# Values and keys of an attention stage as three products of upper and lower parts, in a hybrid decoder step

## The reference

```
z   = x @ w_in                                # 384 query latents | 256 kv latents | 32 rope
ckv = rms_norm(z[..., 384:640], kv_norm)
q   = (rms_norm(z[..., :384], q_norm) @ w_q_up)   # 16 heads x (64 + 32)
s   = q_nope . (ckv @ w_uk[h]) + rope(q) . rope(k), causal, softmax -> p
out = (p @ (ckv @ w_uv[h])) @ w_o
```

## Time and profile before

| what | value |
|---|---|
| median of 3 executions | 1387.92 us (lowest 1387.88) |
| the profiled execution: time | 1389.12 us |
| the profiled execution: span in the trace | 1387.0 us |
| PE busy | 1366.7 us, 99% of the span |
| DVE, ACT, POOL busy | 643.7, 518.8, 258.5 us (46%, 37%, 19%) |
| mean granted TensorE clock | 0.997 |

### The profile page before, as it was taken

The page is one execution under the profiler, slowest core; times in us unless marked ns, Lnnn a source line. Parts: engine busy times, 40 slices in busy tenths (PEclk is TensorE's granted clock), DMA queues, the critical chain, the costliest instruction groups (busy, mean ns, idle before and its releaser), DMA issues.

```text
span 1387.0 us, 26630 instructions
## 1 busy us (share of the span) xinstructions
PE 1366.7 (99%) x10422; PEld 1281.9 (92%) x10422; DVE 643.7 (46%) x934; ACT 518.8 (37%) x838; POOL 258.5 (19%) x350
## 2 busy tenths in 40 slices
PE   9999999999999999999999999999999999999997
PEld 9867777669999999999999999999999999999996
DVE  4556666433752232133233778877432322333335
ACT  4256666332442221122223388854422212222224
POOL 0052222001550000000003415665400000000033
PEclk9999999999999999999999999999999999999998
DMA  8231110242233332222332213132223322332301
GB/s 223 65 97 30 30 22 14 67 148 61 66 87 91 102 99 86 62 79 73 102 126 69 69 36 101 62 115 71 79 75 102 126 61 61 91 90 88 110 1 65
DMA packets 180867, 111.13 MB, mean 80 GB/s; under 512 B 25928, under 2 KB 179101, under 8 KB 180800
## 3 DMA queue, kind: packets, MB, share of 16 engines
q1 hardware_dynamic: 180208, 109.41, 27.1%
q0 software_dynamic: 592, 0.79, 0.2%
HBM read 107.15 MB, written 3.02 MB: 79 GB/s over the span
## 4 chain that ended last, share of the span: by engine, by line
PE 90%; DVE 5%; ACT 2%; issue 1%; SPq 0%; POOL 0%; DMA 0%; DVEq 0%; ACTq 0%; POOLq 0%
PE ps L556 55%; PE ps L585 8%; PE ps L648 4%; PE ps L837 3%; PE ps L850 2%; PE ps L810 1%; PE ps L873 1%; PE ps L1163 1%; PE ps L827 1%; PE ps L1052 1%; PE ps L1215 1%; PE ps L919 1%; PE ps L1074 1%; PE ps L1015 1%; PE ps L1186 1%
## 5 line engine op out<-in xcount | busy, mean ns | idle before, releaser
L556 PE MATMUL ps<-xh,wl 128*128 128x280 f32 x1472 | 310.5, 292 | 0.0
L556 PE MATMUL ps<-xh,wh 128*128 128x280 f32 x1472 | 308.8, 291 | 0.7 <-ACT sg L1579 0.7
L556 PE MATMUL ps<-xl,wh 128*128 128x280 f32 x1472 | 307.8, 290 | 0.0
L1284 ACT ACTIVATE wh<-raw 128x2048 fp32r<-128x2048 f32 (+2 forms) x78 | 161.1, 2065 | 198.6 <-PE ps L556 179.5
L556 PEld LDWEIGHTS ps<-xh,wh 128*128 128x128 f32 x1472 | 233.9, 188 | 1.3 <-ACT sg L1579 1.1
L556 PEld LDWEIGHTS ps<-xh,wl 128*128 128x128 f32 x1472 | 234.6, 189 | 0.0
L1669 DVE TENSOR_TENSOR wl<-raw,wh 128x2048 fp32r<-128x2048 f32 (+2 forms) x78 | 195.9, 2511 | 79.1 <-ACT wh L1284 79.0
L556 PEld LDWEIGHTS ps<-xl,wh 128*128 128x128 f32 x1472 | 232.1, 188 | 0.0
L2033 DVE TENSOR_TENSOR ht<-sg,ps 128x560 f32<-128x560 f32 x44 | 32.5, 738 | 268.9 <-PE ps L556 264.8
L2228 POOL TENSOR_TENSOR acc<-xT 128x560 f32<-128x560 f32 x4 | 7.7, 1933 | 745.7 <-DVE xT L1919 648.5
L1581 ACT ACTIVATE hh<-ht 128x560 f32 (+1 forms) x44 | 29.6, 672 | 262.1 <-DVE ht L2033 262.1
(11 more groups left out here) (361 smaller groups left out, 2576.4 us busy)
## 6 DMA issues: line engine op xcount, KB each, us to landing
raw<-in_ffn_w_gu SPq DMA_DIRECT2D x176, 256.0 KB, 3.7
raw<-in_ffn_w_down SPq DMA_DIRECT2D x48, 384.0 KB, 4.2
raw<-in_lru_w_in SPq DMA_DIRECT2D x16, 512.0 KB, 4.6
Ctok<-in_cache_latent SPq DMA_DIRECT2D x48, 128.0 KB, 2.2
raw<-in_mla_w_o SPq DMA_DIRECT2D x16, 256.0 KB, 3.7
raw<-in_ffn_w_down SPq DMA_DIRECT2D x16, 256.0 KB, 5.1
raw<-in_lru_w_o SPq DMA_DIRECT2D x16, 256.0 KB, 3.4
wq<-in_mla_w_q_up SPq DMA_DIRECT2D x16, 144.0 KB, 2.3
```

Of the source, the lines that this page charges most:

```text
L556: mm = pe.matmul(ps[:, 1024 * jp + 512 * h:1024 * jp + 512 * h + TH], w[:, k, col:col + P], x[:, k, h * TH:(h + 1) * TH], start=(k == 0 an ...
L1284: act.activation(wh[u][:, 0:w], raw[u][:, 0:w], ACT.Copy).then_inc(hi_ok, 1)
```

## The change

The values of token tiles 1 to 4 and all keys are computed from parts, as three products with float32r operands, in place of one float32 product. For this:

- ACT makes `wuvh` and DVE `wuvl`, each 128 x 2048, in the two `raw` buffers (these are free from the split of chunk 1 and of chunk 2 on). The load of `wuv` signals `in_cst` now; waits on `in_att` and `in_cst` are renumbered.
- ACT makes `kvh` and DVE `kvl` of the two normed kv latent tiles, in the places of tiles 6 and 7 of `xh` and `xl`. DVE first waits for the end of chunk 2 (`t1_ok` 3).
- POOL makes `wukh` and `wukl` for each pair, in `key_weights(p)`. `keys(p)` waits for `s_kp2` in place of the load. POOL's start is put in another order: the two first `swap`s and `key_weights(0)` come ahead of the copies into `K` and of the rows out.
- SP waits for all ten groups of values (`s_v` 10) ahead of samples 2 and 3, since their pages overwrite `wuvh` and `wuvl`.

The semaphore counts that moved with it (`s_z`, `s_zroot`, `s_kp2`, `d_new`) follow from these. Diff, with unchanged lines cut:

```
@@ -197,6 +197,12 @@
+        wuvh = place("wuvh", [P, KC, HEADS * VH], F32R, raw_at + 4 * W_MAX)[0]
+        wuvl = place("wuvl", [P, KC, HEADS * VH], F32R, raw_at)[0]
+        wuk_parts = raw_at + 4 * (W_MAX + PAGES * KV_R)
+        wukh, wukl = (place(f"wuk{s}", [P, KC, P], F32R, wuk_parts + 4 * KC * P * i)[0] for i, s in enumerate("hl"))
+        kvh, kvl = (t[:, KD - KC:KD, :] for t in (xh, xl))
+
         Ctok = [put(f"Ctok{s}", [P, PAGES, KV_R]) for s in range(2)]
@@ -419,7 +425,7 @@
             sp.dma_start(trig[:], c_trig).then_inc(in_att, 16)
-            sp.dma_start(wuv[:], mla_w_uv[0].rearrange("(k p) h v -> p k (h v)", p=P)).then_inc(in_att, 16)
+            sp.dma_start(wuv[:], mla_w_uv[0].rearrange("(k p) h v -> p k (h v)", p=P)).then_inc(in_cst, 16)
             sp.dma_start(pages[:], page_table.rearrange("b n -> (b n)").rearrange("(a n) -> a n", a=1)).then_inc(in_pg, 16)
@@ -466,6 +472,7 @@
             sp.wait_ge(lo_ok, 3)
+            sp.wait_ge(s_v, 10)
             for b in range(2, 4):
@@ -780,7 +787,7 @@
-            pe.wait_ge(in_att, 32)
+            pe.wait_ge(in_cst, 48)
             pe.wait_ge(s_z, KC)
@@ -807,8 +814,17 @@
                     for k in range(KC):
-                        mm = pe.matmul(ps[0:n, bank:bank + 512], z[:, KQ + k, kt * P:kt * P + n],
-                                       wuv[:, k, h * 512:(h + 1) * 512], start=(k == 0), stop=(k == KC - 1))
+                        if kt == 0:
+                            mm = pe.matmul(ps[0:n, bank:bank + 512], z[:, KQ + k, kt * P:kt * P + n],
+                                           wuv[:, k, h * 512:(h + 1) * 512], start=(k == 0), stop=(k == KC - 1))
+                            continue
+                        if g == 2:
+                            pe.wait_ge(s_ste, 2)
+                            pe.wait_ge(s_z, KC + k + 1)
+                        for i, (x, w) in enumerate(((kvh, wuvh), (kvl, wuvh), (kvh, wuvl))):
+                            mm = pe.matmul(ps[0:n, bank:bank + 512], x[:, k, kt * P:kt * P + n],
+                                           w[:, k, h * 512:(h + 1) * 512], start=(k == 0 and i == 0),
+                                           stop=(k == KC - 1 and i == 2))
                     mm.then_inc(s_v, 1)
@@ -819,13 +835,15 @@
-                pe.wait_ge(wuk_in, (p + 1) * 16)
+                pe.wait_ge(s_kp2, p * 2 + 4)
                 if above_zero(p):
...
                     for k in range(KC):
-                        mm = pe.matmul(ps[:, 512 * (6 + h):512 * (6 + h) + NP // 2], wuk[:, k, :],
-                                       z[:, KQ + k, h * (NP // 2):(h + 1) * (NP // 2)], start=(k == 0), stop=(k == KC - 1))
+                        for i, (w, x) in enumerate(((wukh, kvh), (wukh, kvl), (wukl, kvh))):
+                            mm = pe.matmul(ps[:, 512 * (6 + h):512 * (6 + h) + NP // 2], w[:, k, :],
+                                           x[:, k, h * (NP // 2):(h + 1) * (NP // 2)], start=(k == 0 and i == 0),
+                                           stop=(k == KC - 1 and i == 2))
                 mm.then_inc(k_sum, 1)
@@ -975,14 +993,14 @@
             pe.wait_ge(s_lte, 2)
-            pe.wait_ge(s_z, 2 * KQ + KC)
+            pe.wait_ge(s_z, 2 * KQ + 2 * KC)
             for n in range(2):
...
             pe.wait_ge(s_vd, 5)
-            pe.wait_ge(s_kp2, 2)
+            pe.wait_ge(s_kp2, 4)
             pe.wait_ge(s_cb, 3)
@@ -994,7 +1012,7 @@
             pe.wait_ge(q_rot, HEADS)
-            pe.wait_ge(in_att, 64)
+            pe.wait_ge(in_att, 48)
             pe.wait_ge(d_new, 3)
@@ -1320,6 +1338,10 @@
                 act.activation(zsq[:, tile, :], z[:, tile, :], ACT.Square).then_inc(s_zsq, 1)
+                if c == 1:
+                    act.wait_ge(in_cst, 48)
+                    act.wait_ge(lo_ok, 2)
+                    act.activation(wuvh[:], wuv[:], ACT.Copy).then_inc(s_parA, 1)
                 act.wait_ge(f1_ok, c + 1)
@@ -1332,6 +1354,9 @@
             act.activation(zsq[:, 2, :], z[:, 2, :], ACT.Square).then_inc(s_zsq, 1)
+            for k in range(KC):
+                act.wait_ge(s_z, k + 1)
+                act.activation(kvh[:, k, :], z[:, KQ + k, :], ACT.Copy).then_inc(s_zroot, 1)
             def row_tile(t):
@@ -1355,7 +1380,7 @@
                     for k in range(KQ):
-                        act.wait_ge(s_z, KC + k + 1)
+                        act.wait_ge(s_z, 2 * KC + k + 1)
                         act.activation(zqh[k][:], z[:, k, :], ACT.Copy).then_inc(s_zroot, 1)
@@ -1738,12 +1763,14 @@
+            dve.wait_ge(s_parA, 2)
+            dve.tensor_tensor(wuvl[:], wuv[:], wuvh[:].bitcast(F32), ALU.subtract).then_inc(s_ste, 1)
             latents(1)
...
                 dve.tensor_scalar(halves(stat[:, n, :]), pair(jp), EPS, None, ALU.add).then_inc(s_zeps, 1)
-                dve.wait_ge(s_zroot, n + 1)
+                dve.wait_ge(s_zroot, 1 + n * (1 + KC))
                 dve.reciprocal(stat[:, n, :], stat[:, n, :]).then_inc(s_zinv, 1)
@@ -1752,7 +1779,7 @@
             normed(0, 2, range(KQ, KQ + KC))
-            dve.wait_ge(in_att, 32)
+            dve.wait_ge(in_att, 48)
             dve.wait_ge(t0_ok, 3)
@@ -1760,6 +1787,10 @@
                 dve.tensor_tensor(krs[r:r + 32, :], rt[:, 0, :], rt[:, 1, :], ALU.add).then_inc(s_kr, 1)
+            dve.wait_ge(t1_ok, 3)
+            for k in range(KC):
+                dve.wait_ge(s_zroot, 2 + k)
+                dve.tensor_tensor(kvl[:, k, :], z[:, KQ + k, :], kvh[:, k, :].bitcast(F32), ALU.subtract).then_inc(s_z, 1)
             for g in range(1, 10, 2):
@@ -1770,7 +1801,7 @@
                     for k in range(KQ):
-                        dve.wait_ge(s_zroot, 3 + k)
+                        dve.wait_ge(s_zroot, 3 + KC + k)
                         dve.tensor_tensor(zql[:, k, :], z[:, k, :], zqh[k][:].bitcast(F32), ALU.subtract).then_inc(s_z, 1)
@@ -2136,7 +2167,7 @@
-            pool.wait_ge(in_cst, 32)
+            pool.wait_ge(in_cst, 48)
             pool.wait_ge(in_id, 16)
@@ -2144,11 +2175,9 @@
             pool.wait_ge(s_cb, 3)
-            pool.wait_ge(s_z, KQ + KC)
+            pool.wait_ge(s_z, KC)
             pool.tensor_copy(zn[:], z[:, KQ:KQ + KC, NP:T]).then_inc(d_new, 1)
-            pool.wait_ge(d_new, 1)
-            for s in range(2):
-                pool.tensor_copy(K[s][64:P, :], krs[64:P, 0:NP]).then_inc(s_kp2, 1)
+            pool.memset(Qs[:], 0.0).then_inc(d_new, 1)
@@ -2163,9 +2192,6 @@
-            for t in range(2):
-                rows_out(t)
-
             def swap(h, u):
@@ -2185,11 +2211,26 @@
-            pool.wait_ge(s_kp2, 2)
-            pool.memset(Qs[:], 0.0).then_inc(d_new, 1)
+            def key_weights(p):
+
+                pool.wait_ge(wuk_in, (p + 1) * 16)
+                if p > 0:
+                    pool.wait_ge(k_sum, p)
+                pool.tensor_copy(wukh[:], wuk[:]).then_inc(s_kp2, 1)
+                pool.wait_ge(s_kp2, 1 if p == 0 else p * 2 + 3)
+                pool.tensor_tensor(wukl[:], wuk[:], wukh[:].bitcast(F32), ALU.subtract).then_inc(s_kp2, 1)
+
             for u in range(2):
...
                 swap(u, u)
+            key_weights(0)
+            pool.wait_ge(s_z, KQ + 2 * KC)
+            pool.wait_ge(s_kp2, 2)
+            for s in range(2):
+                pool.tensor_copy(K[s][64:P, :], krs[64:P, 0:NP]).then_inc(s_kp2, 1)
+            for t in range(2):
+                rows_out(t)
+            pool.wait_ge(s_kp2, 4)
             pool.wait_ge(s_ve, 5)
@@ -2199,6 +2240,7 @@
             swap(2, 0)
+            key_weights(1)
             for h in range(1, HEADS):
@@ -2208,6 +2250,8 @@
                         rows_out(t)
+                elif h % 2 == 0 and h < HEADS - 2:
+                    key_weights(h // 2 + 1)
                 if h < HEADS - 1:
```

## The result

The changed kernel takes 1394.11 us (median of 7), the kernel before 1388.28 us (median of 7 on the same chips). The ratio is 1.0042, 95% interval 1.0031 to 1.0053: slower by 5.8 us, clear of noise and far inside 2%. 1395.1 us was forecast. One execution of each kernel (1482.47 and 2220.05 us) was in a slow state and is left out of the ratio.

A forecast was written before the change was run, and what follows sets the result against it. PE, busy 99% of the span, was taken to bound the kernel. SP's wait +7.1, clock +2.2, keys 1 to 7 -2.1 gave +7.2 us: span 1394.2, median 1395.1 us, range 1389.5 to 1400.

The forecast's parts named there:

- The large term, SP's wait: SP's work behind its new wait makes PE's queries of head 2 +7.1 us late, PE waiting some 10.5 us.
- Values: Value tiles 1 to 4: 48 products take 10.8 us in place of 14.03, -3.2 us, cancelled out by PE's wait.
- Keys: Each of 8 key calls on PE gets 0.3 us shorter; keys 1 to 7 count in the total.
- Clock: PE's clock drops in the new gap and dense work behind it runs at half rate: 2.2 us lost (1.0 to 3.0).
- Sum: All terms on the profiled span: +7.2 us, span 1394.2, median 1395.1 us; ends +4.9 and +11.3.
- Hidden parts: Operand splits on DVE and ACT, POOL's new order and its key weights finish ahead of need: nil.
- The wait costs nothing: Rival, chance 0.08: SP's wait delays nothing and only PE's saving stays, -5.6 us, 1382.3 us.
- Part of the wait: Rival, chance 0.12: SP's wait stalls PE half as long, 5 us, too short for a long clock drop: +0.8, 1388.7 us.
- POOL in DVE's way: Rival, chance 0.07: POOL's key-weight subtraction slows DVE's scaling or query read at each pair, +3.2 us, 1398.3 us.

The follow-up runs named there:

- experiment 1: The kernel before with only SP's new wait for the ten value groups added ahead of samples 2 and 3: 1399.31 us, ratio 1.0079.
- experiment 4: The changed kernel with the 16 page numbers of samples 2 and 3 read ahead of SP's new wait: 1384.1 us, ratio 0.9969.
- experiment 6: The changed kernel with only sample 2's page numbers read ahead of SP's new wait: 1390.3 us, ratio 1.0015.
- experiment 9: The changed kernel with float32 values, no value-weight split or new SP wait, and POOL's key-weight cast and subtraction done twice: 1386.47 us, ratio 0.9987.
- experiment 5: The changed kernel with page numbers read ahead of SP's wait and head 2's query weight loaded between samples 2 and 3: 1382.71 us, ratio 0.9964.
- experiment 7: The changed kernel with 38 unused float32 products of ones on PE ahead of the queries of head 2: 1395.0 us, ratio 1.0048.
- experiment 8: The changed kernel with 46 unused float32 products of ones on PE ahead of the queries of head 2: 1394.39 us, ratio 1.0044.

## Why the prediction was right, step by step

- **The large term, SP's wait.** Forecast: released at 75.3, first page 80.1, last 93.15, weight load 94.0, POOL 97.0, PE 99.35, 10.5 us of stall. In the trace: 74.65, 79.45, 92.50, 93.53, 95.94, 98.17, 9.97 us. This execution started 0.96 us earlier; with that taken out the queries come at 98.17 + 0.96 - 92.28 = +6.85 us late, +7.1 forecast. Two small errors cancel in it: the load of the weight was issued 0.5 us later than forecast, 0.3 of it from the values, and landed in 2.4 and not 3.0 us. Experiments 1, 4 and 6 show the mechanism: the wait alone makes the loss, and taking all or half of the reads from behind it takes the stall off or halves it.
- **Values.** -3.2 us forecast for the 48 products. Measured: 3.00 us for tile 1 and 8.44 us for the others, 11.4 in place of 14.03, -2.6, which is less than my lower bound of -2.7. The step was 0.231 us, between my 0.225 and the proportional 0.235, and the first product behind other work came on top twice, 0.2 and 0.1 us, which I had left out. Another 0.2 us came from the step between `mean_squares` and the values, -2.8 in all (15.1 for 17.9 us). None of this is in the sum, as the stall follows the values. The 0.216 us of the Trainium skill's formula (TensorE: Matmul & The Clock Gate, "Back-to-back issue gap") is too short by 0.015, as it was by 0.010 at 280 columns.
- **Keys.** -0.31 us per pair (20.21 for 20.52 us between calls), -0.3 forecast; 0.1215 us between products of 264 columns, 0.122 forecast. The wait for DVE ahead of them stayed at 0.32, so the whole gain passed.
- **Clock.** The mis-sized term: +2.2 us forecast, 1.05 in the profiled execution, 1.95 in a second one. I took 5 us at half rate from the end of the kernel before. After the release the half rate went on for 3.0 us of work in the first trace of this kernel and for 5.3 in the second, and for 3.2 to 5.1 us in the four other kernels with a stall of over 2 us. So 5 us was a fair guess at a length that changes from execution to execution. The price of it was too high: the stretch lost about a third of the time at half rate (1.05 of 3.0, 1.95 of 5.3), and I had put 2.2 of 5.
- **Sum.** Forecast +7.1 + 2.2 - 2.1 = +7.2. Measured terms +6.85 + 1.05 - 2.2 = +5.7, net span +6.0, medians +5.8. In the second trace +7.3 + 1.95 - 2.2 = +7.1, net span +7.1. So the terms account for both executions within 0.3 us, and the forecast lies at the upper end of what single ones show. The ends of the range for the first term, +6 and +8.3, are a little wider than the errors named for it give.
- **Hidden parts.** `wuvl` ran from 39.30 for 2.28 us, both `kvl` were done by 60.3, the copies into `K` at 71.3: all ahead of their users, as said. `key_weights` took 1.2 to 1.4 us per pair with 0.3 to 0.5 us to spare ahead of `values`, and none needed (experiment 9).
- **Rivals.** "The wait costs nothing" is what experiments 4 and 5 build; in the changed kernel it is wrong by 10 us of stall. "Part of the wait" would have needed 5 us of stall; experiment 6 builds it, and there, too, the clock was down for 3.3 us of work, so a stall of this size was not too short for that, while the +1 us that this rival put for it fits (1.05). "POOL in DVE's way": the scaling of 512 columns did take 0.72 to 0.89 us beside POOL in the changed kernel and 0.49 clear of it, which agrees with the port rule of the Trainium skill (SBUF — State Buffer, "Who interferes with whom"). But before had such rows too, and doubling POOL's key weights left the pair at 20.2 us, so it moves nothing here.

## What to carry to other kernels

A wait costs what stands behind it in its queue, the cheap setup steps included: ask which of these need the wait at all, and put the rest ahead of it. Here reading the page numbers ahead of the wait turned a loss of 5.8 us into a gain of 4.4, and one load moved as well gave 5.5. And a buffer that is "free" at the time of use has a next owner, whose whole chain of loads moves with the borrowing.

## What was not expected of the hardware

Reading a page number into a register of SP costs about 0.6 us (16 reads fewer behind the wait made SP's queue 9.45 us shorter in experiment 4), more than issuing the load of that page (16 loads in 8.07 us, 0.5 each). The half rate after a stall lasted differently in two traces of one kernel, 3.0 and 5.3 us of work, for 1.05 and 1.95 us of loss. The drop came also after only 2.2 us of idling, right behind 8.7 us of dense products (experiment 7), while the gaps of 0.84 and 0.97 us (experiments 8 and 4) left the clock at 1.00.

The same warm-up at the kernel's start took 4.75 to 6.34 us. Later groups of eight of these products go at 0.11 us each; the first 28 took 0.22 us each in the kernel before, twice as long, and 0.18 in the changed one. So PE began at half that rate and came up at a different time in each, though the clock column reads 1.00 there. With waits for the first inputs in some traces, the first product of parts started between 14.72 and 16.61 us.
